# The final norm of a two-block transformer kernel: two of four token blocks normed ahead of the last weight load's rounding

## The reference, cut to what matters

```python
h = rmsnorm_2(x, ffn_norm_g[l])
x = x + (jax.nn.silu(h @ w_gate[l]) * (h @ w_up[l])) @ w_down[l]
return rmsnorm_2(x, final_norm_g)

def rmsnorm_2(x, g):
    xf = x.astype(jnp.float32)
    xf = xf * lax.rsqrt(jnp.mean(xf * xf, axis=-1, keepdims=True) + EPS)
    return (xf * g.astype(jnp.float32)).astype(x.dtype)
```

## Time and profile before

| | |
|---|---|
| median of 3 runs | 1196.08 us (1195.7 to 1196.68) |
| the profiled execution | 1196.68 us |
| its span | 1194.8 us |
| PE busy | 1174.9 us, 98% of the span |
| DVE busy | 803.4 us, 67% |
| ACT busy | 587.6 us, 49% |
| POOL busy | 449.5 us, 38% |
| mean granted clock of TensorE | 0.997 of full speed |

### The profile page before, as it was taken

One profiled execution on the slowest core, in us unless ns is written; L12 is line 12 of the kernel. 1 busy time (PEld: TensorE's weight loads), 2 busy tenths in 40 slices (PEclk: granted clock), 3 DMA queues, 4 the chain that ended last, 5 costly groups with the idle time before them and its releaser, 6 DMA issues.

```text
span 1194.8 us, 15712 instructions
## 1 busy us (share of the span) xinstructions
PE 1174.9 (98%) x5744; PEld 978.3 (82%) x5744; DVE 803.4 (67%) x1597; ACT 587.6 (49%) x1027; POOL 449.5 (38%) x266
## 2 busy tenths in 40 slices
PE   9999999999999999999999999999999999999997
PEld 8878778888888887789778787788888888888886
DVE  5779774784717446799981775764356788776686
ACT  6553574477522454548683787423432222224455
POOL 1417453335444324212362676344344344430000
PEclk9999999999999999999999999999999999999999
DMA  8204662202332532242221401523356564655752
GB/s 272 80 34 132 183 181 72 89 18 72 107 113 81 176 106 71 71 161 91 71 40 36 142 1 59 189 76 102 104 209 214 198 215 150 211 197 190 264 187 86
DMA packets 88795, 150.90 MB, mean 126 GB/s; under 512 B 16776, under 2 KB 43528, under 8 KB 88080
## 3 DMA queue, kind: packets, MB, share of 16 engines
q1 hardware_dynamic: 83680, 131.04, 33.5%
q10 hardware_dynamic: 5040, 18.88, 4.3%
HBM read 127.86 MB, written 15.75 MB: 120 GB/s over the span
## 4 chain that ended last, share of the span: by engine, by line
PE 82%; DVE 10%; ACT 3%; POOL 2%; issue 2%; DMA 0%; SPq 0%; DVEq 0%; ACTq 0%; POOLq 0%
PE bank L2108 62%; PE bank L2424 8%; PE bank L2172 2%; PE bank L2204 2%; PE bank L2186 2%; PE bank L2250 2%; DVE sc L1651 2%; DVE m L1647 1%; DVE sqS L1797 1%; POOL w_lo L838 1%; PE bank L2148 1%; PE bank L2289 1%; DVE rp L1397 1%; ACT w_hi L941 0%; DVE mqT L1848 0%
## 5 line engine op out<-in xcount | busy, mean ns | idle before, releaser
L821 POOL TENSOR_TENSOR w_lo<-w_raw,w_hi 128x2048 fp32r<-128x2048 f32 (+3 forms) x67 | 301.9, 4505 | 515.6 <-ACT w_hi L909 458.4
L2108 PE MATMUL bank<-aH,w_hi 128*128 128x512 f32 x832 | 331.2, 398 | 2.6 <-DVE mqT L1848 1.1
L2108 PE MATMUL bank<-aH,w_lo 128*128 128x512 f32 x832 | 324.7, 390 | 0.0
L2108 PE MATMUL bank<-aL,w_hi 128*128 128x512 f32 x832 | 318.1, 391 | 0.0
L909 ACT ACTIVATE w_hi<-w_raw 128x2048 fp32r<-128x2048 f32 (+4 forms) x63 | 117.5, 1865 | 198.9 <-PE bank L2108 178.4
L2108 PEld LDWEIGHTS bank<-aH,w_hi 128*128 128x128 f32 x832 | 157.0, 189 | 33.6 <-issue 4.4
L2108 PEld LDWEIGHTS bank<-aL,w_hi 128*128 128x128 f32 x832 | 156.3, 188 | 33.5
L2108 PEld LDWEIGHTS bank<-aH,w_lo 128*128 128x128 f32 x832 | 156.9, 189 | 27.7
L2108 PE MATMUL bank<-uH,w_hi 128*128 128x512 f32 x192 | 74.9, 390 | 0.3 <-DVE uL L1869 0.2
L2108 PE MATMUL bank<-uL,w_hi 128*128 128x512 f32 x192 | 74.7, 389 | 0.0
L2108 PE MATMUL bank<-uH,w_lo 128*128 128x512 f32 x192 | 74.7, 389 | 0.0
(11 more groups left out here) (392 smaller groups left out, 2328.3 us busy)
## 6 DMA issues: line engine op xcount, KB each, us to landing
w_raw<-in_w_in SPq DMA_DIRECT2D x21, 1024.0 KB, 5.0
w_raw<-in_w_gate SPq DMA_DIRECT2D x22, 512.0 KB, 3.8
w_raw<-in_w_up SPq DMA_DIRECT2D x22, 512.0 KB, 4.8
third_raw<-in_w_down ACTq DMA_DIRECT2D x9, 1024.0 KB, 4.9
w_raw<-in_w_merge SPq DMA_DIRECT2D x8, 1024.0 KB, 4.9
w_raw<-in_w_out SPq DMA_DIRECT2D x8, 1024.0 KB, 5.0
sums_scratch<-third_raw ACTq DMA_DIRECT2D x9, 768.0 KB, 3.7
w_raw<-sums_scratch SPq DMA_DIRECT2D x6, 768.0 KB, 6.6
```

The lines of the kernel that those rows point to most:

```text
L821: pool.tensor_tensor(out=w_lo[:, c % 2, 0:n], in0=w_raw[:, c % 2, 0:n], in1=w_hi[:, c % 2, 0:n].bitcast(F32), op=ALU.subtract).then_inc(w_ ...
L2108: ins = pe.matmul(o, l, r, start=(kk == 0 and operand == ROUNDED and m == 0), stop=(kk == total - 1 and operand == REST), skip_group_check ...
```

## The change

The steps of the norm become functions on ACT (`fin_square`, `fin_root`, `fin_first_half`) beside those on DVE, and `fin_add` now adds one half. On both engines blocks n = 0 and 1 are done, one after the other, at the head of step d = 19 (`STEPS - 1`), ahead of its `down_high` and `down_low`. Behind step 19, the steps of blocks 2 and 3 are interleaved: block 3's first half is added and squared before block 2 is scaled. The wait for the gain (`small_landed`) moves along, and the last of the additions of `m1` is followed by a wait of DVE for its own result. The instructions of PE, POOL and the SP queue and their order are the same as before.

```diff
@@ ACT @@
+            def fin_square(n, half):
+                b = (n + 2) % NB
+                act.wait_ge(fin_sum, 2 * n + half + 1)
+                act.activation(sq[:, half, :], xr[:, b, S * half:S * half + S], ACT.Square,
+                               accum_out=qs[:, half, b:b + 1]).then_inc(fin_sq, 1)
+            def fin_root(n):
+                b = (n + 2) % NB
+                act.wait_ge(fin_bias, n + 1)
+                act.wait_ge(fin_sq, 2 * n + 2)
+                act.activation(rT[:, b:b + 1], qs[:, 1, b:b + 1], ACT.Sqrt, scale=1.0 / D,
+                               bias=qs[:, 0, 4 + b:5 + b]).then_inc(fin_rms, 1)
+            def fin_first_half(n):
+                b = (n + 2) % NB
+                act.wait_ge(fin_inv, n + 1)
+                act.wait_ge(fin_ready, n + 1)
+                act.activation(xr[:, b, 0:S], xr[:, b, 0:S], ACT.Copy, scale=qs[:, 1, 4 + b:5 + b]).then_inc(half_scaled[0], 1)
...
             for d in range(3, STEPS):
+                if d == STEPS - 1:
+                    for n in range(2):
+                        fin_square(n, 0)
+                        fin_square(n, 1)
+                        fin_root(n)
+                        fin_first_half(n)
                 down_high(d)
...
-            for n in range(NB):
-                b = (n + 2) % NB
-                for half in range(2):
-                    act.wait_ge(fin_sum, 2 * n + half + 1)
...
+            fin_square(2, 0)
+            fin_square(2, 1)
+            fin_root(2)
+            fin_square(3, 0)
+            fin_first_half(2)
+            fin_square(3, 1)
+            fin_root(3)
+            fin_first_half(3)
@@ DVE @@
+            def fin_add(n, half):
+                b, i, at = (n + 2) % NB, n % 2, (low_at, high_at)[half]
+                product = "p7" if n < 2 else ("p2", "p3")[half]
+                wait_filled(dve, product, i)
+                plus(xr[:, b, at], bank_of(product, i)[:], xr[:, b, at]).then_inc(fin_sum, 1)
...
             for d in range(3, STEPS):
                 if SUMMED <= d < SEVENTH:
                     down_sums(d)
+                if d == STEPS - 1:
+                    dve.wait_ge(small_landed, 48)
+                    for n in range(2):
+                        fin_add(n, 0)
+                        fin_add(n, 1)
+                        fin_gain(n)
+                        fin_scale(n)
                 down_low(d)
...
-                            plus(at, at, m1[:, i, :])
+                            ins = plus(at, at, m1[:, i, :])
+                            if not extra:
+                                link(ins)
...
-            fin_add(0)
-            fin_add(1)
-            fin_gain(0)
-            fin_scale(0)
-            fin_gain(1)
-            fin_scale(1)
-            fin_add(2)
+            fin_add(2, 0)
+            fin_add(2, 1)
             fin_gain(2)
+            fin_add(3, 0)
             fin_scale(2)
-            fin_add(3)
+            fin_add(3, 1)
             fin_gain(3)
             fin_scale(3)
```

More of the change, by code:

```diff
@@ L1977, in corner, with fin_gain, fin_scale @@
                     empties(plus(at, bank_of(product, i)[:], at), product, i)
+            low_at, high_at = slice(0, S), slice(S, D)
+            def fin_add(n, half):
[3 more added lines that the diff above has]
+                plus(xr[:, b, at], bank_of(product, i)[:], xr[:, b, at]).then_inc(fin_sum, 1)
+            def fin_gain(n):
+                b = (n + 2) % NB
+                dve.wait_ge(fin_sq, 2 * n + 1)
+                dve.tensor_scalar(qs[:, 0, 4 + b:5 + b], qs[:, 0, b:b + 1], 1.0 / D, EPS,
+                                  ALU.mult, ALU.add).then_inc(fin_bias, 1)
+                mult(xr[:, b, low_at], xr[:, b, low_at], gfin[:, low_at]).then_inc(fin_ready, 1)
+            def fin_scale(n):
+                b = (n + 2) % NB
+                dve.wait_ge(fin_rms, n + 1)
+                dve.reciprocal(qs[:, 1, 4 + b:5 + b], rT[:, b:b + 1]).then_inc(fin_inv, 1)
+                dve.wait_ge(fin_inv, n + 1)
+                dve.wait_ge(fin_sum, 2 * n + 2)
+                dve.scalar_tensor_tensor(out=xr[:, b, high_at], in0=xr[:, b, high_at], scalar=qs[:, 1, 4 + b:5 + b],
+                                         in1=gfin[:, high_at], op0=ALU.mult, op1=ALU.mult).then_inc(half_scaled[1], 1)
             extra = [(t, c, i) for t, c in ((2, 1), (2, 0), (0, 1)) for i in range(2)]
```

## The result

| | before | changed |
|---|---|---|
| median of 6 runs each | 1196.33 us (1195.70 to 1196.68) | 1201.62 us (1201.02 to 1202.86) |
| ratio, 95% interval | | 1.0046 [1.0033, 1.0059] |
| the profiled execution | 1196.68 us | 1201.02 us |
| its span | 1194.8 us | 1199.2 us |

The account below looks back on a forecast made before the run. PE was taken to bound the body, with DVE and ACT meeting it at the end. Late step 19 with the shorter tail (+3.77) plus a clock fall (+1.3) gave +5.07 on 1196.08, so 1201.2 us, range 1199.3 to 1202.8.

Parts of the forecast that it names:

- Where the moved work starts, and its length: Blocks 0 and 1 on DVE and ACT: first add at about 1174.80, block 1's scale at 1182.09.
- What waits behind it: Step 19's rounding queues behind both blocks, ends at 1185.64, so PE waits 4.17 us.
- The clock: PE's granted clock falls around its late wait for step 19, costing 1.3 us.
- two forms: Clock fall for PE's last matmuls: wholly behind the wait, losing 1.7 us, or starting 2.5 us into it, losing 0.95.
- From there to the end: PE's last 30 matmuls, then a tail shortened by interleaving (0.40 gain): last scale at 1194.74, +3.77 us without the clock.
- Costs set to nothing: DVE's new wait for `m1`, earlier stores, POOL and DVE's gain wait were all taken as free.
- The sum: Whole kernel: 3.77 + 1.3 = 5.07 us slower, 1201.2 us for the median.
- The clock that holds: Rival at the end: PE waits but its clock does not fall, +3.77, 1199.9 us; chance 0.13.
- the clock that stays low: Rival at the end: low clock through the last matmul, +3.77 + 6.1, up to 1206 us; longer low chance 0.06.
- Two low stretches: Case of the longer-low rival at PE's end: 1.3 + 1.7 in place of 1.3, 1202.9 us; longer low chance 0.06.
- DVE and ACT alone set the end: Rival: PE has room, so not slower, 1196.1 us or 1195.7 with PE on time; chance 0.05.

Follow-up runs that it names:

- PE kept busy: Changed kernel plus 18 extra matmuls (result unused) on PE between step 18's and step 19's matmuls: 1199.80 against 1195.47 us for the kernel before.
- table loaded early: Changed kernel plus one unused single-column root on ACT ahead of the moved squares, loading the root's table earlier: 1199.58 against 1195.47 us for the kernel before.
- tail order only: Kernel before with only blocks 2 and 3 interleaved; blocks 0 and 1 stay behind step 19: 1195.31 against 1195.47 us for the kernel before.
- one block ahead: Changed kernel with only block 0 ahead of step 19, block 1 behind it: 1196.30 against 1195.94 us for the kernel before.
- spread: Changed kernel with block 0 moved ahead of step 18 and block 1 behind step 19: 1195.74 against 1195.94 us for the kernel before.
- blocks ahead only: Changed kernel with blocks 2 and 3 back in the old order, blocks 0 and 1 ahead of step 19: 1201.57 against 1195.47 us for the kernel before.
- the first four experiments: Tail order only, blocks ahead only, PE kept busy and table loaded early, run on one chip in turn with the kernel before, whose median was 1195.47 us.

## Why the prediction was right

- *Where the moved work starts, and its length.* The first add was put 1.15 behind the start of step 18's last low part and came 1.14 behind it; the two scales were put 3.95 and 7.29 behind the first add and came at 3.96 and 7.30. All of it was read from the same instructions in their old places.
- *What waits behind it.* PE was to take up step 19 4.17 us late; it was 4.23. The hand-over from DVE to PE took 0.15 (1184.50 to 1184.65) where 0.06 was taken; the terms ahead of it were 0.03 shorter together.
- *The clock.* The fall was forecast with 1.3 us, the middle of two forms; it took the form of the wait at 575.91, wholly behind the restart. PE's last 29 steps took 1.74 more than before. With the clock at 1.00 behind a late step 19 (PE kept busy, table loaded early) they take 6.70, 0.12 more than before, so 1.62 of the 1.74 are the clock's, close to that form's 1.7. This term of the sum was mis-sized by 0.3. The other 0.12 come with PE's late start and were no term of the sum; most of it is the second matmul, which starts 0.31 behind the first (1184.65, then 1184.96) in place of 0.23. That a fall came, and where, was in part luck: the prediction expected it from two cases of one trace, and the last section shows that the first of these has no fall in three traces of eight, and that a fall can come sooner. The rule of the Trainium skill on the clock (TensorE: Matmul & The Clock Gate, section "HAM oscillation — how this bites in real kernels"), that such matmuls start at the lower clock, would have put it at 0.95 with the stretch at the end of the kernel before; the first matmuls behind the wait still ran at 1.00. At the wait that ends at 574.66 in the same trace they did start at the lower clock (last section). The run with PE kept busy shows the term by itself, at 1.61.
- *From there to the end.* The tail was to be 0.40 shorter and was 0.37. The size was right and the reason half wrong: the prediction said that here the interleaved order pays. With the blocks ahead and the old order the time was the same, so behind a late PE the tail is short in either order; the interleaving gains its 0.34 only where DVE and PE arrive together, as in the kernel before.
- *Costs set to nothing.* The new wait for the last addition of `m1` made DVE's next instruction 0.07 us later against the rounding that it waits for. The next wait of DVE for ACT, ahead of step 18's low part, takes this up (1.94 in place of 2.01), so nothing of it reaches the end.
- *The sum.* 5.07 was forecast, 5.60 measured between the traces and 5.29 between the medians. The 0.53 between 5.07 and 5.60 are the four terms above: 0.06 (late step 19), 0.32 (clock), 0.12 (PE's late start) and 0.03 (tail).
- *The rivals.* The clock that holds did not come in the changed kernel's trace, the clock that stays low neither (it came back after 3.4 us). Two low stretches were put at 1202.9: two of the six runs took 1202.75 and 1202.86 at a mean granted clock of 0.994, but without a trace it stays open where they lost it. That DVE and ACT alone set the end is refuted by the chain, which goes through PE's 30 matmuls, and by the single block, which costs little because it nearly fits.

## What to carry to other kernels

Before work is moved ahead of a step that feeds another engine, read two times for that step: when it is ready and when it is first needed. Their difference (3.68 us here) is the budget; what exceeds it is paid in full: one block of the two cost 0.6 us. On TensorE a wait of several microseconds can cost a stretch at the lower clock on top (4.2 + 1.6 us here). Idle time of an engine is room for work only if what queues behind that work can wait.

## What the runs showed of the hardware that was not expected

Whether the clock falls behind a wait, and when, is not settled by the wait's length. The kernel before fell 0.7 us behind the end of its wait of 2.31 us at 575.91. In the trace of the changed kernel the same wait ends at 574.66, and the clock fell ahead of that, at about 574.4:

```profile
574.00:574.50 0.50, 0.00 (x0) 0.00 (x0) 0.50 (x2) 0.00 (x0) 0.00 (x0) 0.90 0.74 86
574.50:575.00 0.50, 0.34 (x2) 0.34 (x3) 0.50 (x2) 0.00 (x0) 0.00 (x0) 0.50 0.71 90
```

In the trace of the run with the tail order only, PE stands idle as long at the same place, and the clock holds:

```profile
574.48 0.66 PE L2175 MATMUL bank<-ident,ql 128*128 128x128 f32 x4 [2.31 <-DVE skS L1480]
```

```profile
573.00:574.00 1.00, 0.00 (x0) 0.00 (x0) 1.00 (x5) 0.04 (x1) 0.00 (x0) 1.00 0.12 6
574.00:575.00 1.00, 0.52 (x4) 0.42 (x4) 1.00 (x3) 0.00 (x0) 0.00 (x0) 1.00 0.70 131
575.00:576.00 1.00, 0.97 (x11) 0.86 (x9) 1.00 (x3) 0.82 (x2) 0.00 (x0) 1.00 1.03 373
576.00:577.00 1.00, 1.00 (x7) 0.83 (x5) 1.00 (x3) 1.00 (x2) 0.00 (x0) 1.00 1.05 410
```

Of the eight traces, five show a fall there, from 0.3 us ahead of PE's restart (changed kernel) to 1.2 us behind it (one block ahead), and three (tail order only, table loaded early, spread) none, with the same program up to that place but for moved line numbers. The clock also held behind 2.79 us at the end of the run with the table loaded early, and fell behind 4.06 and 4.07, in both some 0.7 us after the restart. Behind PE's last matmul it fell in all eight traces, 2.0 us (one block ahead) to 5.3 us (PE kept busy) later. So a forecast for a wait of 2 to 3 us needs both cases, and one for 4 us needs several places of the fall: one that starts 2.1 us into the wait of 4.06, as in the changed kernel at 574.4, and lasts 3.4 would have left 1.4 us of it to the matmuls, a cost of 0.7 us by this estimate and not 1.62.

The mean granted clock of each run tells a part of the spread. Of the eleven runs of the changed kernel and of the one with the blocks ahead only, the four at 0.994 took 1202.70 to 1202.86 us, the seven at 0.996 to 0.998 took 1200.99 to 1201.66. In the 17 runs of the kernel before beside the first four experiments there is no such order: 1195.12 to 1197.56 at 0.997, 1195.18 to 1198.15 at 0.998, 1195.17 to 1195.71 at 0.999. The cause of that spread stays open.
